# Attention projections of a hybrid decoder in partition groups: keys two a bank, query rotations four a matmul

## The reference, cut to what matters

```
proj = rmsnorm(h) @ w_in                  # cq 384 | ckv 256 | kr 32 | xr 512 | gt 512
q  = (rmsnorm(cq) @ w_uq)                 # 8 heads x 96: 64 plain, 32 to be rotated
kv = (rmsnorm(ckv) @ w_ukv)               # 8 heads x (64 keys + 64 values)
k  = concat(kv keys, kr broadcast to 8 heads)
q, k = rmsnorm(q, q_head_g), rmsnorm(k, k_head_g)     # over the 96 of each head
q[64:], k[64:] = rotate by cos, sin of the position   # pairs i, i + 16
att = causal softmax(q k / sqrt(96)) v
xc = causal conv of xr over 4 tokens
a, b from sigmoid(xc @ w_a), sigmoid(xc @ w_i);  h_t = a_t h_(t-1) + b_t
mix = concat(rmsnorm(att), rmsnorm(h * gelu(gt))) @ w_out
```

## Time and profile before

| what | value |
|---|---|
| median of 3 runs | 979.43 us (979.31 to 980.3) |
| profiled execution | 975.04 us |
| its span | 973.3 us |
| PE busy | 926.4 us (95%) |
| PEld busy | 830.5 us (85%) |
| DVE busy | 723.5 us (74%) |
| ACT busy | 574.3 us (59%) |
| POOL busy | 44.7 us (5%) |
| mean DMA rate | 209 GB/s |

### The profile page before, as it was taken

One profiled execution on the slowest core, in us unless ns is written; L12 is line 12 of the kernel. 1 busy time (PEld: TensorE's weight loads), 2 busy tenths in 40 slices (PEclk: granted clock), 3 DMA queues, 4 the chain that ended last, 5 costly groups with the idle time before them and its releaser, 6 DMA issues.

```text
span 973.3 us, 15493 instructions
## 1 busy us (share of the span) xinstructions
PE 926.4 (95%) x5838; PEld 830.5 (85%) x5838; DVE 723.5 (74%) x955; ACT 574.3 (59%) x793; POOL 44.7 (5%) x82
## 2 busy tenths in 40 slices
PE   5999989999999999999899899999999999999994
PEld 4974769999999999864778798989899989999993
DVE  5665867666666555656855788979897989799993
ACT  5456454544444344455552787686767777777671
POOL 4240010000000000000012000000000000000000
PEclk9999989999999999999979899999999999999997
DMA  9503212555559653404105389989997999899971
GB/s 279 166 14 106 70 44 87 174 165 177 175 172 245 173 172 104 130 30 143 56 12 195 101 318 353 334 314 355 358 339 288 372 344 350 295 345 361 336 280 46
DMA packets 120024, 203.84 MB, mean 209 GB/s; under 512 B 5874, under 2 KB 73740, under 8 KB 119964
## 3 DMA queue, kind: packets, MB, share of 16 engines
q1 hardware_dynamic: 119504, 202.81, 60.7%
q10 hardware_dynamic: 460, 0.23, 0.1%
HBM read 201.98 MB, written 1.05 MB: 209 GB/s over the span
## 4 chain that ended last, share of the span: by engine, by line
PE 80%; DVE 13%; ACT 4%; issue 2%; DMA 0%; ACTq 0%; DVEq 0%
PE ps L2338 22%; PE ps L2363 11%; PE ps L609 10%; PE ps L611 10%; PE ps L610 10%; DVE wlo L1318 4%; PE ps L1972 2%; PE ps L2296 2%; PE ps L2003 2%; PE ps L2109 1%; ACT whi L892 1%; PE ps L1902 1%; PE ps L2350 1%; PE ps L2311 1%; PE ps L2021 1%
## 5 line engine op out<-in xcount | busy, mean ns | idle before, releaser
L1318 DVE TENSOR_TENSOR wlo<-raw,whi 128x1536 fp32r<-128x1536 f32 (+4 forms) x296 | 437.7, 1507 | 84.2 <-ACT whi L892 82.4
L892 ACT ACTIVATE whi<-raw 128x1536 fp32r<-128x1536 f32 (+4 forms) x296 | 376.3, 1284 | 161.6 <-PE ps L611 84.8
L609 PE MATMUL ps<-uhi,whi 128*128 128x272 f32 (+1 forms) x576 | 169.3, 294 | 3.9 <-DVE ulo L1336 3.9
L611 PE MATMUL ps<-uhi,wlo 128*128 128x272 f32 (+1 forms) x576 | 166.9, 290 | 0.0
L610 PE MATMUL ps<-ulo,whi 128*128 128x272 f32 (+1 forms) x576 | 166.5, 289 | 0.0
L2338 PE MATMUL ps<-whi,xeh 128*128 128x320 f32 (+1 forms) x512 | 124.6, 324 | 0.0
L2338 PE MATMUL ps<-wlo,xeh 128*128 128x320 f32 (+1 forms) x512 | 123.4, 322 | 0.0
L2338 PE MATMUL ps<-whi,xel 128*128 128x320 f32 (+1 forms) x512 | 123.3, 322 | 0.0
L609 PEld LDWEIGHTS ps<-uhi,whi 128*128 128x128 f32 (+1 forms) x576 | 108.9, 189 | 6.7 <-issue 4.9
L610 PEld LDWEIGHTS ps<-ulo,whi 128*128 128x128 f32 (+1 forms) x576 | 109.2, 190 | 0.3
L611 PEld LDWEIGHTS ps<-uhi,wlo 128*128 128x128 f32 (+1 forms) x576 | 108.9, 189 | 0.0
(11 more groups left out here) (302 smaller groups left out, 1327.2 us busy)
## 6 DMA issues: line engine op xcount, KB each, us to landing
raw<-in_moe_w_down_dram SPq DMA_DIRECT2D x24, 1536.0 KB, 7.5
raw<-in_moe_w_gate_dram SPq DMA_DIRECT2D x16, 1536.0 KB, 7.2
raw<-in_moe_w_up_dram SPq DMA_DIRECT2D x16, 1536.0 KB, 8.6
raw<-in_moe_w_gate_dram SPq DMA_DIRECT2D x16, 1280.0 KB, 7.1
raw<-in_moe_w_up_dram SPq DMA_DIRECT2D x16, 1280.0 KB, 6.5
raw<-in_ffn_w_gate_dram SPq DMA_DIRECT2D x11, 1024.0 KB, 5.4
raw<-in_ffn_w_up_dram SPq DMA_DIRECT2D x11, 1024.0 KB, 5.3
raw<-in_ffn_w_down_dram SPq DMA_DIRECT2D x8, 1408.0 KB, 7.1
```

The source lines that it names most:

```text
L609: pe.matmul(dst, wh, xh, start=start, stop=False, skip_group_check=True)
L611: return pe.matmul(dst, wl, xh, start=False, stop=stop, skip_group_check=True)
L892: act.activation(placed(whi, s, src), src, ACT.Copy).then_inc(hi_done, 1)
L1318: dve.tensor_tensor(placed(wlo, s, src), src, placed(whi, s, src).bitcast(F32), ALU.subtract).then_inc(lo_done, 1)
```

## The change

Heads write their own groups of partitions, so that several share one PSUM bank.

- Queries: the rotated 32 columns of four heads go to one block (`qro`, two blocks, 24 matmuls of 32 columns, each head on its own 32 partitions), the plain 64 columns of two heads to one (`qn`, four blocks, 24 matmuls of 64 columns). Two `qro` and two `qn` stand before the gate products, two `qn` behind.
- Rotation: one matmul of 128 columns per `qro` block (`rot`, two in place of eight), issued right after `krr`, before the keys. DVE multiplies by sine and cosine on 128 partitions and adds head by head into `qT`.
- Keys: two heads to one block (`kn`, four blocks, 16 matmuls of 64 columns).
- ACT copies the plain parts of queries and keys head by head on 64 partitions and squares a whole block at once.
- `latss` and `qkss` write 32 columns each to partition groups of their own: two groups for `latss`, four for `qkss` (16 matmuls).
- DVE's reciprocal of `qkss` and the key scaling now stand before the recurrence's product and its four scans, which come after `gelu_gate(0)`; on ACT the root of `qkss` stands before the recurrence's square root and the third value copy.
- The query gain on the plain part moves to the keys (`gqk`, one POOL operation at the start); a 14th small DMA brings the gain for the rotated part (`q_rope_g`); tables of sine and cosine are made on 128 partitions.

```diff
+                def query_block(b, heads, at, width):
+                    fill(pe, b)
+                    for k in range(QC):
+                        for i, h in enumerate(heads):
+                            c = h * QKH + at
+                            q = pe.matmul(bank(b, slice(width * i, width * (i + 1))), wq[:, k, c:c + width], cq[:, k, :],
+                                          start=(k == 0), stop=(k == QC - 1), skip_group_check=True)
+                    q.then_inc(filled, 1)
...
+                for j in range(2):
+                    query_block(B[l, "qro", j], range(4 * j, 4 * j + 4), NOPE, ROPE)
+                query_pairs(range(2))
...
-                queries(range(NH // 2, NH))
+                query_pairs(range(2, NH // 2))
...
+                for j in range(2):
+                    b, raw_q = B[l, "rot", j], B[l, "qro", j]
+                    fill(pe, b)
+                    pe.wait_ge(emptied[raw_q.bank], raw_q.before + 1)
+                    pe.matmul(bank(b), con[:, C_ROT:C_ROT + P], ksq[:, 4 + j, :], start=True, stop=True).then_inc(filled, 1)
...
-                for h in range(NH):
-                    b = B[l, "kn", h]
+                for j in range(NH // 2):
+                    b = B[l, "kn", j]
                     fill(pe, b)
                     for k in range(KVC):
-                        at = h * (NOPE + VH)
-                        q = pe.matmul(bank(b, slice(0, NOPE)), wkv[:, k, at:at + NOPE], ckv[:, k, :],
-                                      start=(k == 0), stop=(k == KVC - 1))
+                        for i in range(2):
+                            at = (2 * j + i) * (NOPE + VH)
+                            q = pe.matmul(bank(b, slice(NOPE * i, NOPE * (i + 1))), wkv[:, k, at:at + NOPE], ckv[:, k, :],
+                                          start=(k == 0), stop=(k == KVC - 1), skip_group_check=True)
...
+                for part in range(4):
+                    for g in range(NH // 2):
...
+                        q = pe.matmul(ps[ROPE * g:ROPE * (g + 1), b.bank, 0:T], w, sq, start=(part == 0), stop=(part == 3),
+                                      skip_group_check=True)
...
 ACT:
+                def pairs(name, dst, sq, js):
+                    for j in js:
+                        b = B[l, name, j]
+                        act.wait_ge(filled, b.ready())
+                        for i in range(2):
+                            act.activation(dst[0:NOPE, 2 * j + i, :], bank(b, slice(NOPE * i, NOPE * (i + 1))), ACT.Copy)
+                        act.activation(sq[:, j, :], bank(b), ACT.Square).then_inc(emptied[b.bank], 1)
...
                 value_block(1)
                 decay_tanh()
-                value_block(2)
-
+                root_rows(B[l, "qkss"], P)
                 act.wait_ge(s_done, l + 1)
                 act.activation(ta[:, :, :], ta[:, :, :], ACT.Sqrt, scale=0.25).then_inc(root_done, 1)
-                root_rows(B[l, "qkss"], 2 * NH)
+                value_block(2)
...
 DVE:
-                for h in ROT_WITH[0] + ROT_WITH[1]:
-                    rotated(h)
+                for j in range(2):
+                    b = B[l, "rot", j]
+                    dve.wait_ge(filled, b.ready())
+                    dve.tensor_tensor(ksq[:, 6 + j, :], bank(b), sinT[:, :], ALU.mult).then_inc(emptied[b.bank], 1)
+                    link(dve.tensor_tensor(ksq[:, 4 + j, :], ksq[:, 4 + j, :], cosT[:, :], ALU.mult))
+                    for i in range(4):
+                        g = slice(ROPE * i, ROPE * (i + 1))
+                        q = dve.tensor_tensor(qT[r, 4 * j + i, :], ksq[g, 6 + j, :], ksq[g, 4 + j, :], ALU.add)
...
-                for h in ROT_WITH[2]:
-                    q = rotated(h)
-                link(q)
-                dve.tensor_tensor(qT[r, :, :], qT[r, :, :], ksq[r, :, :], ALU.add).then_inc(qrot_done, 1)
-
-                dve.wait_ge(root_done, l + 1)
...
-                rows(l, "qk", 2 * NH)
+                rows(l, "qk", P)
...
                 gelu_gate(0)
+                dve.wait_ge(root_done, l + 1)
+                dve.tensor_tensor(tb[:, :, :], tb[:, :, :], ta[:, :, :], ALU.mult).then_inc(b_done, 1)
+                dve.wait_ge(b_done, l + 1)
+                for c in range(CH):
+                    dve.tensor_tensor_scan(xc[:, c, :], decay[:, c, :], tb[:, c, :], 0.0, ALU.mult, ALU.add)
```

More of the change, by code:

```diff
@@ L207, in plan_blocks @@
                 add("kvbc", bank=5)
-        for h in range(NH // 2):
-            add("uq", h)
+        for b in range(2):
+            add("qro", b)
+        for j in range(2):
+            add("qn", j)
         for n in ("wa", "wi"):
@@ L979, in _, with query_ropes @@
                         tables()
[L981 to L985, removed]
+                def query_ropes():
+                    for j in range(2):
+                        b = B[l, "qro", j]
                         act.wait_ge(filled, b.ready())
-                        act.activation(qT[r, h, :], bank(b, r), ACT.Copy, scale=col("q_head_g", l, 0, r))
-                        act.activation(u32[r, h, :], bank(b, r), ACT.Square).then_inc(emptied[b.bank], 1)
-                queries(range(NH // 2))
+                        act.activation(ksq[:, 4 + j, :], bank(b), ACT.Copy, scale=col("q_rope_g", l))
+                        act.activation(u32[:, 4 + j, :], bank(b), ACT.Square).then_inc(emptied[b.bank], 1)
+                def pairs(name, dst, sq, js):
[5 more added lines that the diff above has]
+                        act.activation(sq[:, j, :], bank(b), ACT.Square).then_inc(emptied[b.bank], 1)
+                query_ropes()
+                pairs("qn", qT, u32, range(2))
                 act.wait_ge(hba_done, 1)
@@ L1017, in value_block @@
                     take(B[l, "v", t], vt[:, t, :], cols=slice(0, DH2))
-                queries(range(NH // 2, NH))
-                for h in range(NH):
-                    b = B[l, "kn", h]
[L1023 to L1026, removed]
+                pairs("qn", qT, u32, range(2, NH // 2))
+                pairs("kn", kT, ksq, range(NH // 2))
                 mark().then_inc(ksq_done, 1)
@@ L1953, in _ @@
                         pe.wait_ge(squares, (2 + CH) * l + 2)
-                        parts = [(c, slice(0, P), (C_LATQ if c < QC else C_LATK, 2)) for c in range(QC + KVC)]
-                        sums(b.bank, lambda c: u32[:, c, :], parts).then_inc(filled, 1)
+                        for c in range(QC + KVC):
+                            k, second = divmod(c, 2)
+                            n, at = (KVC, C_LATK) if second else (QC, C_LATQ)
+                            q = pe.matmul(ps[ROPE * second:ROPE * (second + 1), b.bank, 0:T], con[:, at:at + ROPE],
+                                          u32[:, QC * second + k, :], start=(k == 0), stop=(k == n - 1), skip_group_check=True)
+                        q.then_inc(filled, 1)
                     if (name, c) == ("xr", 2):
@@ L1991, in _ @@
                 pe.wait_ge(krg_done, l + 1)
-                pe.matmul(bank(b, r), rot, kr[r, 1, :], start=True, stop=True).then_inc(filled, 1)
+                pe.matmul(bank(b, r), con[r, C_ROT + NOPE:C_ROT + QKH], kr[r, 1, :], start=True, stop=True).then_inc(filled, 1)
+                for j in range(2):
+                    b, raw_q = B[l, "rot", j], B[l, "qro", j]
+                    fill(pe, b)
+                    pe.wait_ge(emptied[raw_q.bank], raw_q.before + 1)
+                    pe.matmul(bank(b), con[:, C_ROT:C_ROT + P], ksq[:, 4 + j, :], start=True, stop=True).then_inc(filled, 1)
                 n = MIX0[l] + UKV
```

133 lines of the change are left out of this document (60 added, 73 removed).

## The result

The changed kernel takes 963.36 us (median of 4 runs, 959.22 to 966.68) against 979.5 for the kernel before (979.31 to 980.3): ratio 0.9842, 95% interval 0.981 to 0.9874, so 15.5 us less. The prediction was 958.8, range 953 to 968. The profiled execution is the slowest of the four, 966.68, span 964.8; that of before was faster than its median, so the two traces differ by only 8.5.

A forecast was written before the change was run, and what follows sets the result against it. PE was taken to bound the mixers first, DVE second. Savings of 10.3 + 10.9 + 1.8, less 0.35 and 2, make 20.65 off 975.04: 954.4, or 958.8 as median; range 953 to 968.

The forecast's parts named there:

- Overlap of partition groups: PE's packed matmuls: four groups run abreast, a qro block's 24 records taking 1.4 us, qkss 1.8, latss 1.5.
- Rival A: Packed matmuls on PE: two groups abreast at most, a qro block 2.8 us, total 964; chance 0.14.
- rival B: Packed matmuls on PE: no overlap for these shapes, a qro block 5.5 us, total 1000; chance 0.06.
- The path to key scaling: Layer 0 mixer: PE's keys, ACT's decay, DVE's products and reciprocal; key scaling starts at 31.6 against 44.8, 13.2 less.
- Layer 1: Layer 1 mixer: key scaling at 32.4 against 45.9, maxima at 42.9 against 53.8, 10.9 us less.
- The clock: Behind the maxima: PE's idle gap brings a lower clock, costing 1 us a layer (bounds 0 and 3), 2 in all.
- Rival C: Clock falls before the reciprocal's end, staying low over key spreads and gt 1: 2 to 4 a layer, 963 to 967; chance 0.13.
- not touched: Everything after the mixer: starts when the mixer ends, so the mixer's saving is carried to the program's end.
- 20.65 forecast: Whole program: 10.3 + 10.9 + 1.8 - 0.35 - 2 us less than the profiled 975.04, giving 954.4.
- From one execution to the median: Whole program: median 4.4 us above the profiled execution, the same distance kept, so 954.4 becomes 958.8.
- the forecast's own 962: Whole program: upper end of the forecast's own range, 954 to 962 us, given a chance of 0.60.

The follow-up runs named there:

- The key experiment: Every packed key block computed twice, against the changed kernel: 968.88 us, ratio 0.9913 to the kernel before, 3.7 above the changed kernel.
- the qkss one: The 16 matmuls of the sums of squares of queries and keys issued twice, against the changed kernel: 963.9 us, ratio 0.9861 to the kernel before.
- The added matmuls: Changed kernel plus unused 272-column matmuls at scores and values: 957.16 us, ratio 0.979; kernel before plus those in values only: 972.84, ratio 0.9943.
- the unused tensors: Kernel before plus two tensors of 352 and 32 bytes per partition that nothing reads or writes: 985.4 us, ratio 1.0077.
- moved tensors: Changed kernel with sines first and added matmuls, two small tensors moved behind the mixers' tensors: 950.75 us, ratio 0.9718 to the kernel before.
- the repeated run: The changed kernel timed again with no edit: 965.2 us, ratio 0.9867 to the kernel before.

## Why the prediction was right, and where it was off

**Overlap of partition groups: right.** Four groups start within one step of 0.23, from one observed pair. A block of 24 records follows its predecessor by 1.37 (1.4 counted); four blocks take 5.86 (5.7), latss 1.5 (1.5), qkss 2.18 (1.8). Rival A, two abreast, would have shown 2.8 for a block, and rival B 5.5. The Trainium skill's "TensorE: Matmul & The Clock Gate", Part 3, lets a load overlap only where the row group differs; here all use the same 128 rows, and 24 records pass in 1.37. The 24 loads of 0.11 each would take 2.6 one after another. The measurement decides against the rule in that form. The same part's 2.38 times for three column groups is too low here: four groups gave four times (16 records in 0.94 instead of 3.84). One thing I had wrong without harm: a group's queue is not without limit but lets three records wait, and the change never puts more than two of a group in a row.

**The path to key scaling: right in order and nearly in size.** In us after the first query matmul of layer 0:

```
step                 counted   measured
gates start             5.7       5.9
qn end                 12.2      12.6
keys end               17.9      18.8
last tanh ends         25.6      26.2
DVE's products end     28.3      28.8
reciprocal ends        30.0      30.6
key scaling            31.6      32.1
first maxima           42.1      42.7
```

The keys are off most, by 0.9: the last block's wait for DVE's sine product, which I had placed at 17.0, ends at 17.6, and a block's records take 1.14 to the end of the last, not 0.9. Half of that is gone again at key scaling. The key experiment shows that this stretch is on the path; the qkss one shows that its 2 us are hidden; and the order of DVE's scans, counted as a plain edit of the change, is worth 6.5 of the 19. The other 12.5 are the packing and two rotations in place of eight together; no run parts these.

**Layer 1: 9.3 of 10.9.** Its key scaling came at 33.5 (32.4 counted). In its chain ACT's table load (1.28, at 417.27) stands between two halves of the gates, as in the kernel before, and the second query blocks end 14.0 after the first query matmul, against 12.6 in layer 0. I had counted 0.8 for what sets layer 1 back; it is 1.4. From key scaling to the maxima it took 11.0, where 10.5 were counted. This is read from the chain; no run took it apart.

**The clock: the mechanism was right, and its size hangs on what is compared.** I saw PE's gap between gt and the maxima, forecast the lower clock behind it and took 1 us a layer, bounds 0 to 3, for what the change adds. The added matmuls give back 7.5 us, and the kernel before was already paying 5.6. By the medians the change thus adds about 2, as counted, but the intervals leave anything from -3 to 7; between the two profiled executions it is more, some 5 (below). Two things were missed. The values stage, much larger than the scores, runs at 1.2 GHz too, and there no exponentials cover it: PE is busy 12.67 of 13.00 us. And the cost differs between executions: most of the scatter goes with the added matmuls. Rival C had the amount (963 to 967) with the wrong place: the spreads in front of key scaling ran at full clock (0.93 for four in both layers, the pace counted).

**What no step held: the addresses.** I wrote that what follows the mixer "is not touched". Its instructions are not, but its tensors moved by 384 bytes. This is the term that the sum lacked: it stands at nothing there. The experts' stage lost 3.7; the unused tensors put the whole cost at 7.5 in the kernel before, and moved tensors gave 4 back.

**How the two profiled executions close.** Of the 20.65 forecast, 2.2 is missing in the mixers' own stages, 3.7 in the experts', and 7.1 behind the maxima; 0.85 came better ahead of the queries, which the repeated run does not show again. That leaves 8.5. Of the 7.1, some 2.2 go to the addresses if they cost there what the unused tensors cost (1.4 + 0.8), the other 5 to the clock. That split is inferred. Between medians less is missing: 15.5 less, or 13.0 by the repeated run, where 20.65 were counted. The mixers' 2.2 and 4 to 7.5 for the addresses are enough for these 5 to 8, with the clock's term as it stands. This too is inferred, and the clock's interval alone (-3 to 7) is wide enough to hide the rest.

**From one execution to the median.** I added 4.4 to get from the profiled execution of before to its median. The changed kernel's profiled execution happened to be its slowest, 3.3 above the median, so the medians differ by 15.5 to 16 and the traces by 8.4. Both scatters go with the clock: the kernel before, in 21 executions from 974.6 to 982.9, had a profiled one at a mean clock of 0.98. A forecast from one execution inherits that scatter.

**The range** held because it reached up to A and C; the time lies 1.4 above the forecast's own 962, and neither A nor C put it there. That is the luck of a wide range: most of what filled it was in none of its terms.

## What to carry to other kernels

Narrow fp32 matmuls are worth splitting by output partition groups with the contraction chunk outermost, but look where the time is given back: at the stretch in which PE now waits for another engine, and whether a few matmuls of no use keep its clock up there. When a change grows a tensor that others are allocated behind, hold the addresses fixed, or measure the shift by itself with an unused tensor: here it cost up to half of what the change brought.

## Not expected of the hardware

- **Addresses in SBUF.** 384 bytes further on, the same 512-column matmul takes 397 ns instead of 392 and the program 7.5 us more (0.8%), with no instruction changed.
- **Four groups abreast at full pace,** 0.235 us a step with all loads from the same rows, and a queue of three records behind the one that starts: four records of a group in a row cost nothing, six leave three groups abreast (8.36 us instead of 5.86 for 72 records).
- **Added work that shortens the program.** Thirty matmuls whose result nobody uses (12 at the scores, 18 in the values) took 7.5 us off it, and most of its scatter.
